# First layers' ends in smaller steps, state-space sums over all 128 rows: a four-layer hybrid kernel on one core

## The reference

```python
ys = jax.nn.gelu(s5_ssm(u, ...))                       # 512 channels: 4 blocks of 128
y_ssm = (ys * jax.nn.sigmoid(ys @ w_ssm_glu[i])) @ w_ssm_o[i]
merged = gates[:, :, 0] * y_attn + gates[:, :, 1] * y_conv + gates[:, :, 2] * y_ssm
x = x + merged @ w_mix_o[i]
```

```python
acs = jnp.cumsum(lac, axis=1)
seg = acs[:, :, None] - acs[:, None, :]
lmat = jnp.where(mask, jnp.exp(jnp.where(mask, seg, 0.0)), 0.0)
y = jnp.einsum('bijgr,bjgrp->bigrp', cb[..., None] * lmat, xc)
```

## Time and profile before

| | |
|---|---|
| median of 3 runs | 2417.84 us (2416.71 to 2418.31) |
| the profiled execution | 2417.19 us |
| its span, first to last instruction | 2415.4 us |
| mean granted clock of TensorE | 0.978 of 2.4 GHz |
| busy: TensorE, VectorE, ScalarE | 95%, 72%, 47% |

### The profile page before, as it was taken

The page is one execution under the profiler, slowest core; times in us unless marked ns, Lnnn a source line. Parts: engine busy times, 40 slices in busy tenths (PEclk is TensorE's granted clock), DMA queues, the critical chain, the costliest instruction groups (busy, mean ns, idle before and its releaser), DMA issues.

```text
span 2415.4 us, 47041 instructions
## 1 busy us (share of the span) xinstructions
PE 2287.6 (95%) x18328; PEld 2202.5 (91%) x18328; DVE 1728.2 (72%) x2691; ACT 1134.8 (47%) x1660; POOL 0.3 (0%) x5
## 2 busy tenths in 40 slices
PE   6799899999998999999999999999999999989998
PEld 6798799998887999989989889999899998889998
DVE  7877777788777776677694567776686765577765
ACT  5243354452433544544635664544545546645443
POOL 0000000000000000000000000000000000000000
PEclk9899899999998999999999999999999999999999
DMA  5233355553333555554344335555554354345554
GB/s 188 89 108 126 115 189 183 172 185 120 106 130 114 187 187 185 194 173 159 123 157 158 114 116 195 198 182 196 190 182 134 132 169 132 112 157 182 183 184 165
DMA packets 104540, 378.57 MB, mean 157 GB/s; under 512 B 11584, under 2 KB 13760, under 8 KB 103872
## 3 DMA queue, kind: packets, MB, share of 16 engines
q1 hardware_dynamic: 102944, 369.14, 46.2%
q10 hardware_dynamic: 1440, 7.19, 0.8%
HBM read 375.23 MB, written 1.05 MB: 156 GB/s over the span
## 4 chain that ended last, share of the span: by engine, by line
PE 59%; DVE 8%; ACT 1%; issue 1%; DVEq 0%; ACTq 0%
PE acc L578 17%; PE acc L580 17%; PE acc L579 17%; DVE w_lo L1436 2%; PE acc L652 1%; PE mid L941 1%; PE acc L653 1%; PE acc L654 1%; PE mid L957 1%; ACT w_hi L1062 1%; PE mid L970 1%; PE mid L943 1%; PE mid L854 1%; DVE pr L2071 1%; DVE xdt L2033 0%
## 5 line engine op out<-in xcount | busy, mean ns | idle before, releaser
L1436 DVE TENSOR_TENSOR w_lo<-w_raw,w_hi 128x1024 fp32r<-128x1024 f32 x699 | 853.0, 1223 | 372.2 <-ACT w_hi L1062 366.0
L1062 ACT CAST w_hi<-w_raw 128x1024 fp32r<-128x1024 f32 x699 | 731.3, 1048 | 620.9 <-PE acc L580 573.9
L578 PE MATMUL acc<-h_hi,w_hi 128*128 128x256 f32 x2128 | 624.3, 293 | 21.4 <-DVE w_lo L1436 12.7
L579 PE MATMUL acc<-h_lo,w_hi 128*128 128x256 f32 x2128 | 609.1, 286 | 0.0
L580 PE MATMUL acc<-h_hi,w_lo 128*128 128x256 f32 x2128 | 608.4, 286 | 0.0
L578 PEld LDWEIGHTS acc<-h_hi,w_hi 128*128 128x128 f32 x2128 | 415.5, 195 | 31.0 <-DVE w_lo L1436 15.7
L578 PE MATMUL acc<-g_hi,w_hi 128*128 128x256 f32 x1488 | 421.9, 284 | 2.6 <-DVE w_lo L1436 2.4
L580 PE MATMUL acc<-g_hi,w_lo 128*128 128x256 f32 x1488 | 420.1, 282 | 0.0
L579 PE MATMUL acc<-g_lo,w_hi 128*128 128x256 f32 x1488 | 418.0, 281 | 0.0
L579 PEld LDWEIGHTS acc<-h_lo,w_hi 128*128 128x128 f32 x2128 | 415.9, 195 | 0.6
L580 PEld LDWEIGHTS acc<-h_hi,w_lo 128*128 128x128 f32 x2128 | 415.1, 195 | 0.0
(11 more groups left out here) (375 smaller groups left out, 3411.5 us busy)
## 6 DMA issues: line engine op xcount, KB each, us to landing
w_raw<-weights_d SPq DMA_DIRECT2D x700, 512.0 KB, 3.3
p<-p_d ACTq DMA_DIRECT2D x3, 1080.0 KB, 8.4
rdec<-decay_d ACTq DMA_DIRECT2D x2, 768.0 KB, 6.7
p<-p_d ACTq DMA_DIRECT2D x1, 1072.0 KB, 9.1
x<-x_d SPq DMA_DIRECT2D x2, 512.0 KB, 5.3
out_d<-work SPq DMA_DIRECT2D x4, 256.0 KB, 2.2
c<-c_d ACTq DMA_DIRECT2D x1, 512.0 KB, 11.1
c<-c_d ACTq DMA_DIRECT2D x1, 448.0 KB, 10.4
```

What stands on the lines that cost most here:

```text
L578: mm(dst, wh, hi[:, k, :], start=first and j == 0, stop=False)
L579: mm(dst, wh, lo[:, k, :], start=False, stop=False)
L1062: nc.scalar.copy(w_hi[:, slot, :], w_raw[:, slot, :]).then_inc(hi_done, 1)
L1436: tt(w_lo[:, slot, :], w_raw[:, slot, :], w_hi[:, slot, :].bitcast(F32), SUB).then_inc(lo_v, 1)
```

## The change

In the task list, the last chunk's `turn`, `cx` and `ssm_y` come one slab earlier (46, 49, 50), gelu two slabs earlier (50) and `ys_lo` too (51). The last `ssm_y` signals each block; ScalarE loads the table of gelu, does gelu and cast for each block of 256 columns in turn, and then loads the table of sigmoid; VectorE makes `ys_lo` by blocks, and slab 54 waits for one block at a time. `slab_k4` now runs over the blocks outside and the two halves inside. `branch_slabs` does the first two blocks of slabs 56 and 57, then the last two of both. `mixed_slabs` does blocks 0 to 3 of slabs 60, 61 and 62, then 4 and 5 of each, then 6 and 7. In the second layers the product of `sums` goes over 128 rows, the lower 64 of which are filled with zeros (two fills on VectorE), and both heads' products come ahead of the four with the mask.

```diff
--- before.py
+++ after.py
@@ -147,14 +147,15 @@
         for j in range(4):
             put(i + 1 + j, ("rot", c, j))
         put(i + (4 if c == NCH - 1 else 5), ("scan", c))
-        put(i + 6, ("turn", c))
-        put(i + 9, ("cx", c))
-        put(i + 10, ("ssm_y", c))
+        last = c == NCH - 1
+        put(i + (5 if last else 6), ("turn", c))
+        put(i + (8 if last else 9), ("cx", c))
+        put(i + (9 if last else 10), ("ssm_y", c))
     for c, i in enumerate((11, 20, 30, 41)):
         for j in range(4):
             put(i + j, ("bu", c, j))
-    put(52, ("gelu",))
-    put(53, ("gelu_lo",))
+    put(50, ("gelu",))
+    put(51, ("gelu_lo",))
     for h in range(HEADS):
         i = (15, 17, 24)[h // 3]
         put(i, ("scores", h))
@@ -423,6 +424,8 @@
         pe_y = sem("pe_y")
         v_y = sem("v_y")
         a_gelu = sem("a_gelu")
+        v_yb = sem("v_yb")
+        a_yshi = sem("a_yshi")
         v_yslo = sem("v_yslo")
         pe_v = sem("pe_v")
         a_v = sem("a_v")
@@ -616,13 +619,52 @@
                 bank(at, t)
                 products(at, i, acc[t % 4][:, 0:T], 0, P, range(KD), hi, lo, need=need).then_inc(used, 1)
 
-            def slab_k4(at, i, t, hi, lo):
+            def part_k4(at, i, t, ks, hi, lo, need=None):
+
+                slot = i % RING
+                for k in ks:
+                    if need is not None:
+                        need(k)
+                    for b in range(2):
+                        dst = acc[t % 4][:, b * T:(b + 1) * T]
+                        a = k * 2 * P + b * P
+                        wh, wl = w_hi[:, slot, a:a + P], w_lo[:, slot, a:a + P]
+                        mm(dst, wh, hi[:, k, :], start=k == 0 and b == 0, stop=False, skip_group_check=True)
+                        mm(dst, wh, lo[:, k, :], start=False, stop=False, skip_group_check=True)
+                        done = mm(dst, wl, hi[:, k, :], start=False, stop=k == 3, skip_group_check=True)
+                return done
+
+            def slab_k4(at, i, t, hi, lo, need=None):
 
                 weights_of(at, i)
                 bank(at, t)
-                for b in range(2):
-                    done = products(at, i, acc[t % 4][:, b * T:(b + 1) * T], b * P, 2 * P, range(4), hi, lo)
-                done.then_inc(used, 1)
+                part_k4(at, i, t, range(4), hi, lo, need).then_inc(used, 1)
+
+            def branch_slabs(at, i):
+
+                for n in range(2):
+                    weights_of(at, i + n)
+                    bank(at, i + n)
+                    part_k4(at, i + n, i + n, (0, 1), yv_hi, yv_lo, lambda k: pe.wait_ge(v_yvlo, at.n * 2 + 1))
+                for n in range(2):
+                    part_k4(at, i + n, i + n, (2, 3), yv_hi, yv_lo, lambda k: pe.wait_ge(v_yvlo, at.n * 2 + 2)).then_inc(used, 1)
+
+            def mixed_slabs(at, i):
+
+                for ks in ((0, 1, 2, 3), (4, 5), (6, 7)):
+                    for n in range(3):
+                        if ks[0] == 0:
+                            weights_of(at, i + n)
+                            bank(at, i + n)
+                        slot, dst = (i + n) % RING, acc[(i + n) % 4][:, 0:T]
+                        for k in ks:
+                            pe.wait_ge(v_mlo, at.n * 4 + (k // 2 + 1))
+                            wh, wl = w_hi[:, slot, k * P:(k + 1) * P], w_lo[:, slot, k * P:(k + 1) * P]
+                            mm(dst, wh, h_hi[:, k, :], start=k == 0, stop=False)
+                            mm(dst, wh, h_lo[:, k, :], start=False, stop=False)
+                            done = mm(dst, wl, h_hi[:, k, :], start=False, stop=k == KD - 1)
+                        if ks[-1] == KD - 1:
+                            done.then_inc(used, 1)
 
             def slabs_long(at, i, t, n, blocks, hi, lo, need=None):
 
@@ -687,7 +729,7 @@
                     elif j == 2:
                         pe.wait_ge(v_rope, at.n * 5 + 5)
                 elif q == 3:
-                    pe.wait_ge(v_y, at.n * 4 + c)
+                    pe.wait_ge(v_y, at.n * 3 + c)
                 elif c < 3:
                     pe.wait_ge(v_mask, at.n * 8 + (6 if c == 1 else 8))
                 elif q:
@@ -791,16 +833,18 @@
                         pe.wait_ge(v_olo, at.n * 4 + 4)
                     slab_k4(at, i, i, o_hi, o_lo)
                 elif i < SO0:
-                    if i == GL0:
-                        pe.wait_ge(v_yslo, at.n + 1)
-                    slab_k4(at, i, i, ys_hi, ys_lo)
+                    slab_k4(at, i, i, ys_hi, ys_lo, (lambda k: pe.wait_ge(v_yslo, at.n * N1 + (k + 1))) if i == GL0 else None)
                 elif i < MX0:
                     if i == SO0:
-                        pe.wait_ge(v_yvlo, at.n * 2 + 2)
-                    slab_k4(at, i, i, yv_hi, yv_lo)
+                        branch_slabs(at, i)
+                    elif i > SO0 + 1:
+                        slab_k4(at, i, i, yv_hi, yv_lo)
                 else:
 
-                    slab_k8(at, i, i, (lambda k: pe.wait_ge(v_mlo, at.n * 4 + (k // 2 + 1))) if i == MX0 else None)
+                    if i == MX0:
+                        mixed_slabs(at, i)
+                    elif i > MX0 + 2:
+                        slab_k8(at, i, i)
 
             pe.sem_inc(used, RING)
             for t in range(4):
@@ -937,8 +981,9 @@
                     pe.wait_ge(v_xdt, at.n * 8 + 8)
                     pe.wait_ge(v_dt, at.n * 4 + 4)
                 for n in range(2):
-                    pick = sel[0:2 * SH, 2 * b + n:2 * b + n + 1].to_broadcast([2 * SH, P])
-                    mm(mid[n][:, 0:TRI], pick, sums[0:2 * SH, :], start=True, stop=False)
+                    pick = sel[:, 2 * b + n:2 * b + n + 1].to_broadcast([P, P])
+                    mm(mid[n][:, 0:TRI], pick, sums[:, :], start=True, stop=False)
+                for n in range(2):
                     for lo in (0, T):
                         last = mm(mid[n][:, lo:lo + P], unit[:, :], above[:, :], start=False, stop=lo == T)
                 last.then_inc(pe_bc, 1)
@@ -1175,10 +1220,14 @@
                 last.then_inc(a_exp, 1)
 
             def gelu(at):
-                act.wait_ge(v_y, at.n * 4 + 4)
-                nc.scalar.activation(ysg[:, :, :], u[:, :, :], ACT.Gelu_apprx_tanh).then_inc(a_gelu, 1)
-                act.wait_ge(a_gelu, at.n * 2 + 1)
-                nc.scalar.copy(ys_hi[:, :, :], ysg[:, :, :]).then_inc(a_gelu, 1)
+
+                nc.scalar.preload_act_table(ACT.Gelu_apprx_tanh)
+                for blk in range(N1):
+                    act.wait_ge(v_yb, at.n * N1 + (blk + 1))
+                    nc.scalar.activation(ysg[:, blk, :], u[:, blk, :], ACT.Gelu_apprx_tanh).then_inc(a_gelu, 1)
+                    act.wait_ge(a_gelu, at.n * N1 + (blk + 1))
+                    nc.scalar.copy(ys_hi[:, blk, :], ysg[:, blk, :]).then_inc(a_yshi, 1)
+                nc.scalar.preload_act_table(ACT.Sigmoid)
 
             def probs(at, h):
                 act.wait_ge(pe_t, at.n * 8 + (h + 1))
@@ -1748,9 +1797,12 @@
                 dve.wait_ge(pe_y, at.n * 4 + (c + 1))
                 tokens = slice(c * CH, c * CH + CH)
                 for blk in range(N1):
-                    last = stt(u[:, blk, tokens], u[:, blk, tokens], par1("d", blk, blk + 1),
+                    part = stt(u[:, blk, tokens], u[:, blk, tokens], par1("d", blk, blk + 1),
                                mid[3][:, blk * CH:(blk + 1) * CH], MUL, ADD)
-                last.then_inc(v_y, 1)
+                    if c == NCH - 1:
+                        part.then_inc(v_yb, 1)
+                if c < NCH - 1:
+                    part.then_inc(v_y, 1)
 
             def scores(at, h):
 
@@ -1788,8 +1840,9 @@
                 tt(o_lo[:, a, :], mid[0][:, 0:T], o_hi[:, a, :].bitcast(F32), SUB).then_inc(v_olo, 1)
 
             def gelu(at):
-                dve.wait_ge(a_gelu, at.n * 2 + 2)
-                tt(ys_lo[:, :, :], ysg[:, :, :], ys_hi[:, :, :].bitcast(F32), SUB).then_inc(v_yslo, 1)
+                for blk in range(N1):
+                    dve.wait_ge(a_yshi, at.n * N1 + (blk + 1))
+                    tt(ys_lo[:, blk, :], ysg[:, blk, :], ys_hi[:, blk, :].bitcast(F32), SUB).then_inc(v_yslo, 1)
 
             def conv_lo(at, b):
 
@@ -1932,6 +1985,7 @@
 
             dve.wait_ge(consts2, 16)
             copy(unit[:, :], con1("ident"))
+            nc.vector.memset(sel[2 * SH:P, :].bitcast(F32), 0.0)
             tt(sel[0:2 * SH, :], con1("ident")[0:2 * SH, 0:SH], con1("ident")[0:2 * SH, SH:2 * SH], ADD)
             ts(above[:, :], con2("tri")[:, 0:P], -1.0, 1e30, ADD, MUL).then_inc(v_above, 1)
 
@@ -2001,6 +2055,7 @@
 
                 dve.wait_ge(pe_dt, at.n * 3 + 3)
                 dve.wait_ge(a_dt, at.n * 5 + 5)
+                nc.vector.memset(sums[2 * SH:P, :].bitcast(F32), 0.0)
                 ts(dts[:, 9, :, :], mid[0][:, 2 * SH:4 * SH].rearrange("p (r h) -> p r h", r=2), -1.0, None, MUL)
                 lo = sums[SH:2 * SH, :]
```

## The result

The changed kernel takes 2391.68 us (median of 5 runs, 2390.27 to 2396.14) against 2417.84 for the kernel before, run beside it (5 runs), a ratio of 0.9895 (95% interval 0.9884 to 0.9907); predicted were 2391. The profiled execution took 2390.27 us with a span of 2388.5.

A forecast was written before the change was run, and what follows sets the result against it. The prediction took TensorE, busy 95% of the span, as the bound. First layers 12.8 us plus pairs 14.4 less fills 0.6 gave 26.6 us off, so 2391 us from a median of 2417.84, range 2378 to 2404.

The forecast's parts named there:

- Turning the last chunk back: First layers, turn ahead of slab 50's w_lo: TensorE waits 3.4 us instead of 2.2, slab 53 ends 0.9 us later.
- Gelu by blocks: First layers, 0.77 us a block: slab 54 starts at 272.8 instead of 274.57, VectorE idles 4.9 us before it.
- On the table load: ScalarE's exposed Sigmoid load: 1.28 us by the profile row; the skill's drain would add 1.4 us per layer.
- Output slabs in halves: Slabs 56 and 57: TensorE starts at 282.1 instead of 286.0, first merge at 287.85, 2.85 us won.
- Mixing slabs in parts: Slabs 60 to 62: merges end at 303.2, new 2.7 us stall before slab 62; layer wins 6.4 us.
- The pairs: Second layers, sums and mask products: each pair 0.45 us shorter, 14.4 us over 32 pairs, bounds 9.9 to 19.
- Only the order pays: Rival, chance 0.13: in the pairs the format costs, not the rows; 9.9 us from 32 pairs, 2396 us.
- New waits eat the gain: Rival, chance 0.11: waits ahead of slab 50 and for slab 54's cast cancel the first layers' gain; 2404 us.
- The clock does not come back: Rival, chance 0.03: low clock persists between first-layer stalls, 13 us per layer at its point; the kernel gets slower.
- The signs: Expected waits: ys_lo about 5 us, yv_lo 4 or 5, h_lo near zero, slab 62 2.7, xst up 1.2 a layer.

The follow-up runs named there:

- h: The changed kernel with ScalarE's gelu one slab later, behind slab 54's cast, its table still loaded where gelu was; 2381.18 us, ratio 0.9852.
- a_ends: The kernel before with only the first layers' part of the change, the pairs left as they were; 2403.62 us, ratio 0.9939.
- b_pairs: The kernel before with only the second layers' pairs changed (both sums products first, 128 rows, two fills); 2405.90 us, ratio 0.995.
- d: The kernel before with the pairs' sums products over 128 rows and the fills, but in the old order; 2406.72 us, ratio 0.9959.
- c: The kernel before with the pairs in the new order but still over 64 rows; 2406.43 us, ratio 0.9958.
- f: The changed kernel with the first two output slabs and first three mixing slabs taken whole again; 2404.12 us, ratio 0.9943.
- e_unmoved: The changed kernel with the last chunk's turn, cx, ssm_y and gelu back at their old slabs, blocks and slab parts kept; 2393.73 us, ratio 0.9903.

## Why the prediction was right

The time, 2391.68 us against 2391, came out of errors of opposite sign, and its closeness is luck: the layers gave 4.7 us more than forecast, the rest 3.3 less (10.5 for 13.8), and the piece ahead of the scan took 1.2 back. The direction, the two halves and the chain of steps were right. Step by step, the first layer in the time of before:

- *Turning the last chunk back.* TensorE's `xst` wait was forecast at 3.4 us and is 3.34. The 14 low-clock products behind it did not come: slab 53's end was put at 270.4 and is at 274.24 - 3.71 - 1.19 = 269.3. It changed nothing, since slab 54 was waiting for `ys_lo`.
- *Gelu by blocks.* 0.77 us for a block, measured 0.76 to 0.77 (265.55 to 266.32 for the first). Sigmoid's load and the cast behind it came where they were put, VectorE's idle time was 4.98 us for 4.9, slab 54 started at 273.05 for 272.8. The 15 low-clock products that the text gave slab 54 were 27, 1.1 us more at its 0.094; that too changed nothing, because `yv` was bound by VectorE, as the text had it. The step was right, and h shows what it left lying: the order of two ScalarE tasks.
- *On the table load.* The cast at 270.00 starts 1.29 us behind the load at 268.71, with no more than the load's own 1.28 us between. The Trainium skill (ScalarE: Activation LUTs, What ACT_TABLE_LOAD costs) would have it at 2.66 us with its drain; this load doesn't show it, and the row was the right choice.
- *Output slabs in halves.* The first `yv_lo` was ready at 282.19 for 282.1, the second at 285.65 for 285.5, the merge started at 287.44 for 287.85. TensorE's products behind the wait ran at the full clock, where the text had taken 1.3 us for the low one; only 0.4 of that shows at the merge, since TensorE then waits for the second `yv_lo`. The stall itself, put at 2.1 us, was 0.82 and 0.26, because the low clock of slabs 54 and 55 had filled it.
- *Mixing slabs in parts.* Last `h_lo` at 302.79 for 303.2, the new wait before slab 62 2.49 us for 2.7, slab 68 at 320.39 for 322.1. Again the clock: 15 low products, 1.4 us, were assumed and none seen.

So the first layer won 8.15 us instead of 6.4, and the second, where before has 27 low products behind one stall, 9.3: 17.5 us instead of 12.8. The mis-sized term is the low clock behind the stalls: four stretches of some 15 products were assumed, and one of 27 was there, at a place where it was covered. The text's own upper bound of 9.4 us named the case in which the two later stalls bring none. But that case isn't the code's doing: in the first layer of a_ends, with the same code, both brought it, and the layer won 4.7 us and not 8.15. So the part is worth 14.0 (a_ends) to 17.5 us (after) in the layers, by where the low clock falls, and the forecast of 12.8 lies nearer to the lower one.

- *The pairs.* The mis-sized term is the saving for a pair, 0.37 us (1.04 less 0.67) for 0.45, so 11.8 us for 14.4 in 32 pairs; b_pairs measured 11.9 us in time and 10.5 in the rest of the table. The reasoning held, rows and not format, but its streams were put too short: the two products over `sums` and the step behind them take 0.46 us (1305.98 to 1306.44), where the forecast had 0.16 to 0.18 from one to the other and about as much again. The rest of the pair, 0.21, is what it was taken for. The two fills, put at 0.6 us, can't be told from the scatter.
- *The rivals.* "Only the order pays": fallen, but not as it was argued. d shows that the rows matter, c shows that the order alone gets the same, 0.29 of 0.37 us. They are two ways to one gain. "New waits eat the gain": the two waits came, with their sizes, and no table was called back between the blocks. "The clock does not come back": it came back 27 products behind slab 54's start.
- *The signs.* `xst` up by 1.2 a layer, `h_lo` gone, slab 62's wait and VectorE's 4.98 us were as written. `ys_lo` at 7.4 us for about 5 and `yv_lo` at 2.2 for 4 to 5 were not: TensorE reached slab 54 earlier and slab 56 later than the low-clock terms had it.

## What to carry to other kernels

When steps are cut small so that the next engine can start early, look at what else stands in the queue of the engine that does the small steps: here one cast behind them held back VectorE by 4.98 us, and moving it ahead was worth 3.5 us a layer at slab 62, as much as the mixing slabs' parts. An earlier start pays only if the waits behind it get shorter too (f, where slab 54 starts as early as in after, but the whole slabs behind it wait for their last input and the layer is as long as before). An engine's idle 0.69 us in a chain that repeats is a place for an independent step that is due anyway: it took the merge from 4.18 to 3.06 us. Of the 4.3 us by which the last `h_lo` came earlier TensorE got only 2.2, because the step it waited for had moved behind two others.

## What the runs showed of the hardware

The granted clock behind a stall does not follow from the stall's length. Behind the wait of 2.18 us for `xst` before shows the low level, behind that of 3.33 us after shows none; a window behind each, first of before, then of after:

```profile
259.00:262.00 3.00, 3.00 (x28) 2.83 (x19) 3.00 (x5) 0.00 (x0) 0.00 (x0) 0.50 0.50 173
```

```profile
258.00:262.00 4.00, 3.87 (x71) 3.73 (x61) 4.00 (x5) 0.00 (x0) 0.00 (x0) 1.00 0.53 146
```

Likewise the 2.5 us before slab 62 were followed by 1.00 in after and by 0.50 in e_unmoved, where they come 1.7 us later from the scan on. Nor does it follow from the code: the first layer of a_ends has that of after, with the same stalls of 3.3 us for `xst` and 2.5 before slab 62, and the low clock behind both. And in code that is the same in all these kernels the low clock came and went, 1.4 us at a time, which makes 4 us between after and h_cast_first. What sets it was not tried. A comparison of two spans can't tell such shifts from the effect of an edit. Cutting the spans at marks that both kernels have takes out those in other pieces, and the windows' clock shows those in the same piece.
